# Gated networks with three paired steps in place of two, two block products in banks of their own, and another order of the vector and scalar work in the pair

## The reference, cut to what matters

```python
def swiglu(x, w_gate, w_up, w_down):
    return (jax.nn.silu(x @ w_gate) * (x @ w_up)) @ w_down

f = swiglu(rms_norm_2(x, g[0]), ffn_w_gate[layer, 0], ffn_w_up[layer, 0], ffn_w_down[layer, 0])
x = x + 0.5 * rms_norm_2(f, g[1])
```

## Time and profile before

| | us |
|---|---|
| median of 3 runs (lowest and highest) | 1807.3 (1806.36 to 1808.53) |
| the profiled execution's own time | 1802.45 |
| its span, first to last instruction | 1800.1 |
| PE busy in the span | 1755.6 (98%) |
| DVE busy | 1390.0 (77%) |
| ACT busy | 994.9 (55%) |

### The profile page before, as it was taken

The page is one execution under the profiler, slowest core; times in us unless marked ns, Lnnn a source line. Parts: engine busy times, 40 slices in busy tenths (PEclk is TensorE's granted clock), DMA queues, the critical chain, the costliest instruction groups (busy, mean ns, idle before and its releaser), DMA issues.

```text
span 1800.1 us, 25241 instructions
## 1 busy us (share of the span) xinstructions
PE 1755.6 (98%) x10314; PEld 1480.7 (82%) x10314; DVE 1390.0 (77%) x1646; ACT 994.9 (55%) x1206; POOL 58.2 (3%) x98
## 2 busy tenths in 40 slices
PE   9999999999999999999999999999999999999998
PEld 8998898788887887877898988778877878888776
DVE  5349877789898898968498778786887667879684
ACT  5446653577777676545452355545554465655452
POOL 0040000000000001000000000000100010010000
PEclk9999999999999999999999999999999999999999
DMA  9344344699899897364442025527443745143631
GB/s 381 118 166 140 118 142 161 240 353 354 337 354 348 344 366 269 123 275 159 168 165 94 27 76 205 234 95 306 160 191 113 303 164 187 48 164 132 266 152 71
DMA packets 51380, 363.01 MB, mean 202 GB/s; under 512 B 5697, under 2 KB 5825, under 8 KB 8642
## 3 DMA queue, kind: packets, MB, share of 16 engines
q1 hardware_dynamic: 50976, 359.24, 52.6%
q10 hardware_dynamic: 290, 2.17, 0.3%
HBM read 360.34 MB, written 1.05 MB: 201 GB/s over the span
## 4 chain that ended last, share of the span: by engine, by line
PE 76%; DVE 17%; ACT 3%; issue 2%; DMA 1%; POOL 0%; DVEq 0%; POOLq 0%; ACTq 0%
PE bank L2869 8%; PE bank L3427 4%; PE bank L3429 4%; PE bank L3428 4%; DVE w_a L1719 4%; PE bank L3281 3%; PE bank L3283 3%; PE bank L3282 3%; PE bank L3454 3%; PE bank L3452 3%; PE bank L3453 3%; PE bank L2927 3%; PE bank L3298 2%; PE bank L3300 2%; PE bank L3299 2%
## 5 line engine op out<-in xcount | busy, mean ns | idle before, releaser
L1719 DVE TENSOR_TENSOR w_a<-ring,w_a 128x2048 fp32r<-128x2048 f32 x220 | 500.5, 2288 | 148.6 <-ACT w_a L994 148.0
L994 ACT ACTIVATE w_a<-ring 128x2048 fp32r<-128x2048 f32 x219 | 416.1, 1912 | 148.9 <-DMA ring<-in_stream 62.1
L1719 DVE TENSOR_TENSOR w_b<-ring,w_b 128x2048 fp32r<-128x2048 f32 x63 | 144.1, 2287 | 35.9 <-ACT w_b L994 35.8
L994 ACT ACTIVATE w_b<-ring 128x2048 fp32r<-128x2048 f32 x63 | 120.5, 1912 | 46.6 <-DMA ring<-in_stream 25.3
L2869 PE MATMUL bank<-h,w_a 128*128 128x256 f32 x1040 | 137.2, 285 | 1.0 <-DVE ring_lo L1824 1.0
L2869 PEld LDWEIGHTS bank<-h,w_a 128*128 128x128 f32 x1040 | 128.8, 191 | 4.1 <-issue 3.0
L3452 PE MATMUL bank<-w_a,hid 128*128 128x512 f32 x280 | 110.0, 393 | 0.0
L3454 PE MATMUL bank<-w_a,hid 128*128 128x512 f32 x280 | 109.2, 390 | 0.0
L3453 PE MATMUL bank<-w_a,hid 128*128 128x512 f32 x280 | 109.0, 389 | 0.0
L3427 PE MATMUL bank<-w_a,h 128*128 128x512 f32 x240 | 95.0, 396 | 0.5 <-DVE w_a L1719 0.5
L3429 PE MATMUL bank<-w_a,h 128*128 128x512 f32 x240 | 93.7, 390 | 0.0
(11 more groups left out here) (647 smaller groups left out, 4197.7 us busy)
## 6 DMA issues: line engine op xcount, KB each, us to landing
ring<-in_stream SPq DMA_DIRECT2D x330, 1024.0 KB, 5.9
G<-in_gains SPq DMA_DIRECT2D x14, 512.0 KB, 7.4
cmp_area<-in_cmp_w ACTq DMA_DIRECT2D x1, 2048.0 KB, 11.3
sm<-in_small SPq DMA_DIRECT2D x1, 1582.0 KB, 12.0
con<-in_consts SPq DMA_DIRECT2D x1, 1032.0 KB, 16.0
X<-in_x SPq DMA_DIRECT2D x2, 512.0 KB, 3.9
out_x<-X SPq DMA_DIRECT2D x4, 256.0 KB, 2.1
sm<-in_small SPq DMA_DIRECT2D x1, 730.5 KB, 22.5
```

The costliest lines, as they stand in the source:

```text
L994: act.activation(w_slot(unit)[:, 0, :], ring[:, unit % RING, :], ACT.Copy).then_inc(S("w_hi"), 1)
L1719: dve.tensor_tensor(w_slot(unit)[:, 1, :], ring[:, unit % RING, :], w_slot(unit)[:, 0, :].bitcast(FP32), ALU.subtract).then_inc(S("w_lo"), 1)
```

## The change

`PAIRS` becomes `(2, 5, 8)`: steps 2 and 3, 5 and 6, 8 and 9 are pairs; steps 1, 4, 7 and 10 are plain. The sums of the activations are made around step 0's end. The product with b12 gets bank 5 and the product with t4 starts bank 7 anew; DVE adds what they used to accumulate on. The split of unit 3s+2 (b12) goes ahead of that of 3s+1 (the down unit of s-1), and DVE's and ACT's orders in the step before the pair and in the pair are changed.

```diff
-PAIRS = (3, 7)
+PAIRS = (2, 5, 8)
+        def split_place(name, n):
+            if name.startswith("ffn") and (n - 1) // 3 in PAIRS and (n - 1) % 3 < 2:
+                return n + 1 - 2 * ((n - 1) % 3)
+            return n
...
-                LO[unit] = ("w_lo", len(LO) + 1)
+                LO[unit] = ("w_lo", first + split_place(name, n) + 1)
...
-        PAIR_DVE = ["t3", "t2", "t4", "t2_lo", "u2", "t1", "t4_lo", "u3", "c21", ...
+        PAIR_DVE = ["t3", "t2", "t4", "t2_lo", "u2", "t4_lo", "u3", "t1", "c21", ...
@@ ACT, pair
                     silu_of(bank[4], 0)
-                    split_at(3 * s + 4)
                     act.wait_ge(S("ffn_dve"), ffn_at(FFN_DVE, name, f"t1_{i}"))
                     act.wait_ge(S("ffn_pe"), ffn_at(FFN_PE, name, f"m4_{i}"))
                     act.activation(sum_hi[:, :], w_sum, ACT.Copy).then_inc(S("ffn_act"), 1)
                     act.wait_ge(S("ffn_dve"), ffn_at(FFN_DVE, name, f"c21_{i}"))
                     silu_of(c_21, 1)
+                    split_at(3 * s + 4)
                     split_at(3 * s + 5)
@@ ACT, gated
                 silu(0, 1)
+                x_sums_high()
                 split_at(5)
...
                     if s + 1 in PAIRS:
                         pair_ahead(PAIRS.index(s + 1), s + 1)
-                    split_at(3 * s + 4)
-                    split_at(3 * s + 5)
-                    if s + 2 == PAIRS[0]:
-                        x_sums_high()
+                        split_at(3 * s + 5)
+                        split_at(3 * s + 4)
+                    else:
+                        split_at(3 * s + 4)
+                        split_at(3 * s + 5)
@@ DVE, pair
-                    hid_left(s - 1, range(0, 2))
                     dve.wait_ge(S("ffn_act"), ffn_at(FFN_ACT, name, f"m1_{i}"))
                     dve.wait_ge(S("ffn_pe"), ffn_at(FFN_PE, name, f"m6_{i}"))
                     joined(c_12, bank[7], m_1)
+                    split_at(3 * s + 1)
+                    hid_left(s - 1, range(0, 2))
+                    ring_left(f"t4_hi_{i}", b21)
+                    dve.wait_ge(S("ffn_pe"), ffn_at(FFN_PE, name, f"m7_{i}"))
+                    own(f"u2_{i}")
+                    joined(c_22, bank[5], c_12)
+                    hid_made(s, 0)
                     first_sum(i, s)
                     split_at(3 * s + 3)
-                    hid_made(s, 0)
-                    ring_left(f"t4_hi_{i}", b21)
-                    dve.wait_ge(S("ffn_pe"), ffn_at(FFN_PE, name, f"m7_{i}"))
-                    joined(c_22, bank[7], m_1)
-                    split_at(3 * s + 4)
                     dve.wait_ge(S("ffn_pe"), ffn_at(FFN_PE, name, f"m4_{i}"))
-                    joined(c_21, bank[7], m_1)
+                    own(f"u3_{i}")
+                    joined(c_21, bank[7], c_22)
                     sum_left(f"t1_hi_{i}", w_sum_lo, w_sum)
                     hid_made(s, 1, c_21)
+                    split_at(3 * s + 4)
                     dve.wait_ge(S("unit_used"), b22 + 1)
@@ DVE, gated
                 hid_made(0, 0)
                 split(name, 3)
                 split_at(4)
+                x_whole()
                 hid_made(0, 1)
+                x_sums()
                 split_at(5)
+                x_left()
...
                     hid_made(s, 0)
                     hid_left(s - 1, range(0, 2))
                     if ahead is not None:
                         third_sum(ahead, s + 1)
+                        second_sum(ahead, s + 1)
                     split_at(3 * s + 3)
                     hid_made(s, 1)
                     if ahead is not None:
-                        more_weight_sums(ahead, s + 1)
+                        fourth_sum(ahead, s + 1)
                         sum_left(f"t2_hi_{ahead}", w_sum_lo, ...)
+                        split_at(3 * s + 5)
+                        continue
@@ PE, pair
                     product(4, own[1], whole[1], False).then_inc(S("unit_used"), 1)
-                    sum_ready(f"u2_{i}")
                     lo_ready(b12)
-                    product(7, both[2], whole[2], False).then_inc(S("ffn_pe"), 1)
+                    product(5, both[2], whole[2], True).then_inc(S("ffn_pe"), 1)
                     down_ready(s - 1, range(0, 2))
                     down_tile(s - 1, 0)
-                    sum_ready(f"u3_{i}")
-                    product(7, own[2], (sum_hi[:, :], ring_lo[:, b21 % RING, :]), False).then_inc(S("ffn_pe"), 1)
+                    sum_ready(f"t4_lo_{i}")
+                    product(7, own[2], (sum_hi[:, :], ring_lo[:, b21 % RING, :]), True).then_inc(S("ffn_pe"), 1)
```

More of the change, by code:

```diff
@@ L570, in build @@
                             ("ffn2", 3 * FFN_STEPS), ("c", C_SPLIT), ("ffn3", 3 * FFN_STEPS)):
+            first = len(LO)
             for n in range(units):
                 unit = D_UNITS[name] + n
-                LO[unit] = ("w_lo", len(LO) + 1)
+                LO[unit] = ("w_lo", first + split_place(name, n) + 1)
         RELEASE = dict(LO)
@@ L670, in build @@
         FFNS = ["ffn0", "ffn1", "ffn2", "ffn3"]
-        PAIR_DVE = ["t3", "t2", "t4", "t2_lo", "u2", "t1", "t4_lo", "u3", "c21", "t1_lo", "w", "c12", "c22"]
+        PAIR_DVE = ["t3", "t2", "t4", "t2_lo", "u2", "t4_lo", "u3", "t1", "c21", "t1_lo", "w", "c12", "c22"]
         FFN_DVE = ["x_raw", "s1", "s2", "s3", "s4", "s_lo"] + [f"{step}_{i}" for i in range(len(PAIRS)) for step in PAIR_DVE]
@@ L1717, in split @@
                 unit = D_UNITS[name] + n
-                dve.wait_ge(S("w_hi"), SPLIT0[name] + n + 1)
+                dve.wait_ge(S("w_hi"), SPLIT0[name] + split_place(name, n) + 1)
                 dve.tensor_tensor(w_slot(unit)[:, 1, :], ring[:, unit % RING, :], w_slot(unit)[:, 0, :].bitcast(FP32),
@@ L2374, in first_sum, with second_sum @@
                     dve.tensor_tensor(w_sum, ring[:, b22 % RING, :], ring[:, b11 % RING, :], ALU.subtract).then_inc(S("ffn_dve"), 1)
-                def more_weight_sums(i, s):
-                    b11, b21, b12, _ = pair_units(name, s)
+                def second_sum(i, s):
+                    b11, _, b12, _ = pair_units(name, s)
                     own(f"t3_{i}")
@@ L2380, in more_weight_sums, with fourth_sum @@
                     dve.tensor_tensor(ring[:, b11 % RING, :], ring[:, b12 % RING, :], ring[:, b11 % RING, :], ALU.add).then_inc(S("ffn_dve"), 1)
+                def fourth_sum(i, s):
+                    b11, b21, _, _ = pair_units(name, s)
                     own(f"t2_{i}")
@@ L2404, in pair @@
                     joined(c_12, bank[7], m_1)
+                    split_at(3 * s + 1)
[5 more added lines that the diff above has]
+                    hid_made(s, 0)
                     first_sum(i, s)
                     split_at(3 * s + 3)
-                    hid_made(s, 0)
-                    ring_left(f"t4_hi_{i}", b21)
-                    dve.wait_ge(S("ffn_pe"), ffn_at(FFN_PE, name, f"m7_{i}"))
-                    joined(c_22, bank[7], m_1)
-                    split_at(3 * s + 4)
                     dve.wait_ge(S("ffn_pe"), ffn_at(FFN_PE, name, f"m4_{i}"))
-                    joined(c_21, bank[7], m_1)
+                    own(f"u3_{i}")
+                    joined(c_21, bank[7], c_22)
                     sum_left(f"t1_hi_{i}", w_sum_lo, w_sum)
                     hid_made(s, 1, c_21)
+                    split_at(3 * s + 4)
                     dve.wait_ge(S("unit_used"), b22 + 1)
-                    own(f"u2_{i}")
                     joined(c_12, bank[4], c_12)
@@ L2443, in gated @@
                     hid_left(s - 1, range(0, 2))
-                    if s + 2 == PAIRS[0]:
-                        x_whole()
                     if ahead is not None:
                         third_sum(ahead, s + 1)
+                        second_sum(ahead, s + 1)
                     split_at(3 * s + 3)
@@ L2450, in gated @@
                     if ahead is not None:
-                        more_weight_sums(ahead, s + 1)
+                        fourth_sum(ahead, s + 1)
                         sum_left(f"t2_hi_{ahead}", w_sum_lo, ring[:, pair_units(name, s + 1)[0] % RING, :])
+                        split_at(3 * s + 5)
+                        continue
                     split_at(3 * s + 4)
-                    if s + 2 == PAIRS[0]:
-                        x_sums()
                     split_at(3 * s + 5)
-                    if s + 2 == PAIRS[0]:
-                        x_left()
                 hid_made(last, 0)
```

## The result

| | before | after |
|---|---|---|
| median (lowest to highest of 4 runs) | 1806.83 (1802.31 to 1808.53) | 1841.29 (1836.1 to 1844.81) |
| ratio, with its 95% interval | | 1.0192 (1.0162 to 1.0223) |
| the profiled execution, its span | 1802.45, 1800.1 | 1836.1, 1834.3 |

The account below looks back on a forecast made before the run. PE's instruction count and idle stretches, mainly waits for DVE, were taken to bound the kernel. Pairs -29.9, start +41.9, later pairs' loads +7 and clock +1 gave +20 on the 1807.3 median: 1827 us, range 1814 to 1842.

Parts of the forecast that it names:

- The pairs, -29.9: Eight pairs and eight plain steps become twelve pairs of 31.45 us without their long waits: 29.9 us less.
- the walk: Hand timing of each engine's queue through one pair, from M, the start of its second product: 31.45 us a pair.
- The start, +41.9: From step 1 to the first pair's second product, DVE's queue of sums and preparation makes PE late: +41.9 us over four networks.
- Rival 3: Networks' start: the chain of sums and preparation is covered, so the kernel gets faster, 1785 us; chance 0.08.
- The clock inside the start, hidden: Half clock behind the 6 us idles at down(0) costs nothing, as PE then waits for DVE at the first pair's second product.
- Rival 4: Idle at the first pair's second product: the clock falls behind it in each network too, +26 in all, 1833 us; chance 0.12.
- +1: Half clock behind the idle of 1.2 to 3 us at the first pair's second product, at 1 in 8: +1 us.
- Three pairs with one plain step between, +7: Later pairs' third sums wait for the eighth load, making second products 0.9 us late at 8 pairs: +7 us.
- Late next, with 0.3 us in hand: In each pair, hid_left, behind the down unit's load and splits, is ready 0.3 us before PE's down product: no cost.
- Rival 2: The pair's down unit lands late in every pair: 1.2 us x 12, +14 more, 1841 us; chance 0.10.
- Rival 1: Start chain as forecast, but later pairs' third sums find their unit in time: +13, 1820 us; chance 0.14.
- rival 5: The pair's fourth product still waits, for a late t4_lo: +2 x 12, 1851 us; chance 0.03.

Follow-up runs that it names:

- order_3_7: The changed kernel with pairs back at steps 3 and 7 and the activation sums back in step 1: 1784.68 us, 0.9883 of the kernel before.
- order_3_7_t1: The changed kernel with pairs at 3 and 7, activation sums back in step 1, and first_sum made before t4's low part: 1780.71 us, 0.9854 of before.
- pairs_2_7: The changed kernel with only two pairs, at steps 2 and 7: 1826.47 us, 1.0118 of the kernel before.
- sums_early_3_7: The kernel before, pairs at 3 and 7, with only the activation sums moved to the end of step 0: 1848.11 us, 1.0243 of before.
- busy_wait: The changed kernel with 40 unused identity matmuls on PE before each network's first down product: 1841.06 us, 1.0179 of the kernel before.
- t1_early: The changed kernel with first_sum made before t4's low part, so the pair's down unit loads sooner: 1825.22 us, 1.0107 of the kernel before.
- hid_in_first: The changed kernel with ACT's hid_in(s) moved before the split of the down unit's follower: 1829.75 us, 1.013 of the kernel before.
- late_sums: The changed kernel with activation sums placed later, DVE's behind hid_made(0,1), hid_left(0) and hid_made(1,1), ACT's behind hid_in(0): 1830.24 us, 1.0128 of the kernel before.
- late_t1_hid: The changed kernel with later activation sums, first_sum before t4's low part, and hid_in(s) before the follower's split: 1832.44 us, 1.0142 of the kernel before.
- banks_only: The kernel before, its own pairs and order, with only the b12 and t4 products in banks of their own: 1795.38 us, 0.9945 of before.
- half_loads: The changed kernel with most gated-network units loaded only in half their columns: 1831.89 us, 1.0143 of the kernel before.

## Why the prediction was right in its sign and short in its size

The two large terms, the gain of the pairs and the loss at the start, came out as worked out. The 13.3 us that were missing are waits of the later pairs, in two places that were sized too small, and some of the clock.

**The pairs, -29.9: right.** order_3_7 has the terms of this part alone: 8 x 31.45 against 272.82 is -21.2; measured are -20.1, with 3.0 us of waits at down(s). order_3_7_t1, without those, has -25.4, of which the clock has a part. In the change itself the four stretches behind M, less the waits below, are 124.6 to 124.7 us in three networks, where the walk has 124.88.

**The start, +41.9: right within 0.1 us.** M came 122.40 us behind the step's start over four networks, where 122.3 were worked out; the idle in `ffn0` is 1.8, 5.7 and 0.8 us, where 2, 6 and 3 stood. The third is smaller because the down product ran partly at half clock ahead of it, as forecast. The step from order_3_7 to pairs_2_7 has 41.8 us. sums_early_3_7 has 43, which is near by chance: it is made of 28.5 us of waits and of half clock that is paid. Rival 3, a covered start, is out.

**The clock inside the start, hidden: right**, by DVE's unbroken queue up to M; busy_wait agrees but couldn't tell. Rival 4 is out in its form: no half clock followed the idle of 0.6 to 0.8 us at M. But +1 was short, for two stretches of 3.41 us at 0.50 later in `ffn2` (1376.55 and 1403.85), behind idles of 2.11 and 1.96 us, that cost about 3.2.

**Three pairs with one plain step between, +7: the step that was too small.** The eight later pairs' second products came 14.3 us late (3.0, 2.2, 1.6, 1.8, 2.4, 0, 1.5 and 1.8), where 7.2 were worked out. This is counted from start to start, as the walk does; the waits view, which counts from a modelled end of the turn, has 12.6 for the same seven waits. The mechanism was right: the third sum is released by the eighth load, and DVE's 11.6 us follow. The size of the burst was off: the last load landed at M+39.7 in the first gap of `ffn0` and at M+38.1 in that of `ffn1`, where the walk had M+37 to 38. The eight bursts of the change took 23.7 to 25.9 us, against 23.5 and 22.7 in the earlier trace rows. The first load of each has 5.3 to 5.8 us to its landing, once 7.5, instead of 4.7 to 4.8: the pair's own down unit was issued 2.1 us ahead of it, and I had counted from an idle queue. t1_early, with 5.3 us between the two, shows that this is the cause of 0.6 to 1.1 us a burst. What remains is in the burst: loads land one every 2.5 us, but each burst, before and after, has one or two longer pitches (2.9 to 4.4 us in the change, up to 6.1 in the kernel before) whose cause no run isolates.

**"Late next, with 0.3 us in hand", 0: should have been +5.** Rival 2 was the right place with the wrong mechanism. The down unit did land on time (4.7 to 4.9 us in all pairs), but its follower's split stands in ACT's queue ahead of `hid_in(s)`, and the walk has no place for `hid_in(s)` at all. The delays of down(s), start to start, came to 5.0 us in nine places, 0.06 to 2.12 each; the largest, in `ffn2`, is behind the one follower that took 7.5 us to land. t1_early and hid_in_first remove them by two different ways.

Together: 7.1 us at second products (14.3 less 7.2), 5.0 at down products and 2.2 of the clock (3.2 less 1) are 14.3, and the walk was 1.0 too long in the rest: 13.3, which is what was missing. Rival 1, a third sum in time, and rival 5, a fourth product still late, are both refuted by the waits above; pairs_2_7 shows what rival 1 describes only where two more plain steps lie between. The forecast of 1827 is 14 us short, and the measured 1841.29 is just inside the 1842 that ended the range. That end was set for rival 2, a late down unit in every pair, which did not happen: what filled the distance instead is the longer burst, `hid_in(s)` and the clock.

The gains are not additive: t1_early brings 16 us and late_sums 11, but all three repairs 9. The later pairs' waits are tied to each other by the stream of loads, and an earlier M moves the eighth load little. In seven of the eight gaps between pairs of the change the next pair starts when the burst and DVE's sums behind it are done, not when PE is. The clock has its part too, as the 8 us of late_t1_hid. What stays open: the long pitch in each burst, and why half clock follows an idle of 2.0 or 2.1 us in `ffn2` and not the 2.8 us at 800.76.

## What to carry to other kernels

A shorter order for the busiest engine is worth what its walk says only while each other queue still has slack: list, for every buffer that the new order frees later, how many transfers now start together, and count from the first issue, with the transfer that is already on its way. Walk every engine's queue, also of the one that seems to have time: here one copy behind a split that waits for a load cost 5 us. Sums that a first pair needs belong in a step with nothing else to prepare: here moving them one step ahead cost 42 us and undid a gain of 20. Take the good half of a change by itself before judging the whole: the new banks and order, with `first_sum` one place earlier, give 1780.7 us, 1.5% under the kernel before.

## What the runs showed of the hardware

- Idle of PE for 5.7 to 5.9 us was followed by 6.83 us at a granted clock of 0.50 in all four networks, of the change and of late_sums; in sums_early_3_7 one of the four was 3.41 us. With idles of 1.98 us one of eight in the earlier trace rows was followed by 3.41 us, but that execution had a clock of 0.998; most others of the kernel before have 0.993 to 0.997. In the change an idle of 2.11 and one of 1.96 us were followed by 3.41 us, and one of 2.79 us was not. With idles of 1.42 us (banks_only) the clock is 0.998 to 1.000. The Trainium skill ("TensorE: Matmul & The Clock Gate", section "HAM oscillation — how this bites in real kernels") says that a starved PE starts its next burst cold; the long idles agree each time, and the short ones some of the time, more often than the one profile showed.
- Half clock is free while the next thing that PE meets is a wait for DVE (in the change PE still waits 0.57 to 0.84 us at M behind 6.83 us of it), and costs 2.46 us on 36 matmuls of 8.44 us where it is not.
- A unit of 1 MB takes 4.7 to 4.9 us from issue to landing by itself, and 5.3 to 6.1 us, once 7.5, behind one issued 2.1 us earlier; behind one issued 5.3 us earlier it is 4.7 to 5.0 (t1_early). A burst lands one every 2.5 us, but for one or two longer pitches, of 2.9 to 4.4 us in the change. Half a unit (half_loads) takes 3.6 to 3.8 us by itself, and a run of them lands one every 1.3 us.
